# A two-block transformer kernel: heads gated in pairs between mixes, constants made in the down stage, one low half ahead of a head pair

## What is computed

```
# first block
y_att = (_rms(o, subln_w[l]) * (1.0 - lambda_init)).reshape(b, lp, ATT_V)
y_conv = u @ w_conv_out[l]
m = jax.nn.sigmoid(g_att) * y_att + jax.nn.sigmoid(g_conv) * y_conv
h = h + m @ w_out[l]
...
h = h + (jax.nn.silu(gate) * val) @ w_down[l]
# second block
lb_all = jnp.cumsum(jax.nn.softmax(hgrn_lb_logits, axis=0), axis=0)
fg = lbh + (1.0 - lbh) * jax.nn.sigmoid(heads(f, dk))
...
o = o * lax.rsqrt(jnp.mean(o * o, axis=-1, keepdims=True) + EPS)
o = o.reshape(B, S, H * dv) * norm_g
o = o * jax.nn.silu(og)
y_b = o @ w_br_hgrn[l]
```

## Time and profile before

| | |
|---|---|
| median of 3 runs | 1180.97 us |
| the profiled execution's own time | 1181.03 us |
| its span | 1179.4 us |
| TensorE busy | 1134.6 us, 96% of the span |
| VectorE, GpSimd, ScalarE busy | 61%, 55%, 51% |
| chain of waits that ended last, by engine | PE 75%, DVE 10%, issue 7%, POOL 5%, ACT 3% |
| mean granted clock of TensorE | 0.988 |

### The profile page before, as it was taken

The page is one execution under the profiler, slowest core; times in us unless marked ns, Lnnn a source line. Parts: engine busy times, 40 slices in busy tenths (PEclk is TensorE's granted clock), DMA queues, the critical chain, the costliest instruction groups (busy, mean ns, idle before and its releaser), DMA issues.

```text
span 1179.4 us, 24897 instructions
## 1 busy us (share of the span) xinstructions
PE 1134.6 (96%) x8962; PEld 1092.2 (93%) x8962; DVE 720.4 (61%) x1364; ACT 600.3 (51%) x1112; POOL 651.6 (55%) x453
## 2 busy tenths in 40 slices
PE   6999999999889999999899999999999999999997
PEld 6999999998779999999899989898989989999996
DVE  5675766789647777426775757666666546444322
ACT  5654444455256666437545455554635455444332
POOL 5666767660255666544753637364475437656642
PEclk9999999999989999999999999999999999999998
DMA  8444443441344555543432423333445425555541
GB/s 325 144 154 141 171 141 143 143 152 69 142 179 144 178 178 178 199 159 108 178 143 109 142 107 115 134 129 122 160 161 179 143 103 184 181 181 202 185 143 36
DMA packets 26209, 179.43 MB, mean 152 GB/s; under 512 B 2848, under 2 KB 4128, under 8 KB 4768
## 3 DMA queue, kind: packets, MB, share of 16 engines
q1 hardware_dynamic: 25856, 178.28, 42.1%
q10 hardware_dynamic: 288, 0.27, 0.1%
HBM read 177.49 MB, written 1.05 MB: 151 GB/s over the span
## 4 chain that ended last, share of the span: by engine, by line
PE 75%; DVE 10%; issue 7%; POOL 5%; ACT 3%; DVEq 0%; DMA 0%; POOLq 0%; ACTq 0%
PE ps L570 50%; PE ps L852 10%; POOL parts L415 3%; PE ps L930 2%; PE ps L636 1%; DVE ps L2186 1%; DVE act L1824 1%; PE ps L485 1%; ACT parts L1130 1%; DVE branch L1965 1%; PE ps L923 1%; POOL sq L2316 1%; PE ps L610 1%; POOL res L2411 1%; DVE work L1731 1%
## 5 line engine op out<-in xcount | busy, mean ns | idle before, releaser
L415 POOL TENSOR_TENSOR parts<-ring,parts 128x1024 fp32r<-128x1024 f32 x208 | 513.8, 2481 | 468.7 <-ACT parts L1130 465.8
L570 PE MATMUL ps<-x_high,parts 128*128 128x256 f32 (+2 forms) x3088 | 418.0, 284 | 4.3 <-POOL parts L415 2.2
L570 PEld LDWEIGHTS ps<-x_high,parts 128*128 128x128 f32 x3088 | 387.5, 189 | 15.5 <-issue 7.1
L1130 ACT ACTIVATE parts<-ring 128x1024 fp32r<-128x1024 f32 x324 | 323.9, 1049 | 138.3 <-PE ps L852 69.3
L415 DVE TENSOR_TENSOR parts<-ring,parts 128x1024 fp32r<-128x1024 f32 x116 | 152.6, 1315 | 127.3 <-ACT parts L1130 127.3
L570 PE MATMUL ps<-x_low,parts 128*128 128x256 f32 (+2 forms) x1520 | 214.5, 284 | 0.0
L570 PEld LDWEIGHTS ps<-x_low,parts 128*128 128x128 f32 x1520 | 196.3, 189 | 0.0
L1751 DVE SCALAR_TENSOR_TENSOR ps<-glu,table_sb,ps 128x256 f32<-128x256 f32 x232 | 93.3, 481 | 0.6 <-DVE ps L1751 0.3
L852 PE MATMUL ps<-act_high,parts 128*128 128x256 f32 x704 | 87.8, 279 | 0.0
L852 PEld LDWEIGHTS ps<-act_high,parts 128*128 128x128 f32 x704 | 85.1, 188 | 0.0
L570 PE MATMUL ps<-parts,x_high 128*128 128x256 f32 x448 | 62.3, 285 | 0.9 <-DVE work L2099 0.9
(11 more groups left out here) (333 smaller groups left out, 1602.2 us busy)
## 6 DMA issues: line engine op xcount, KB each, us to landing
ring<-weights SPq DMA_DIRECT2D x166, 1024.0 KB, 4.8
res<-h_in SPq DMA_DIRECT2D x4, 272.0 KB, 3.6
act<-mem SPq DMA_DIRECT2D x1, 1024.0 KB, 14.6
out<-xT SPq DMA_DIRECT2D x4, 256.0 KB, 2.4
table_sb<-table SPq DMA_DIRECT2D x1, 969.5 KB, 8.9
table_sb<-table ACTq DMA_DIRECT2D x1, 132.5 KB, 3.5
work<-positions ACTq DMA_DIRECT2D x1, 128.0 KB, 5.5
```

What stands on the lines that cost most here:

```text
L415: eng.tensor_tensor(parts[:, LOW - HIGH + p, cols], ring[:, slot, cols], parts[:, p, cols].bitcast(F32), ALU.subtract)\
L570: mm = pe.matmul(out, left(k), right(k), start=step_ == 0 and k == 0, stop=step_ == 2 and k == KB - 1)
L1130: sc.activation(parts[:, p, cols], ring[:, slot, cols], ACT.Copy).then_inc(split_high, 1)
```

## The change

Three parts. (1) `gate_heads` is split into `root_heads` (the reciprocal) and `gate_heads` (the two multiplications), both for any number of heads. Heads 0 to 3 stay as they were; heads 4 and 5, then 6 and 7, are done in pairs, the reciprocal and the multiplications of a pair at different places between the mixes. (2) The constants and the exponential leave `tables1` and `tables2` and become `constants2` and `bound_exps`, given to `down_low` and `down_high`. (3) In the second block `low_b(2)` stands ahead of `gate_b(3)`.

```
@@ ScalarE, tables2
+            def bound_exps():
+
                 sc.wait_ge(consts_ready, 2)
                 sc.activation(lb_t[:, 0:16], lb_t[:, 0:16], ACT.Exp).then_inc(lb_exp, 1)
...
-            down_high("down1")
+            down_high("down1", bound_exps)
@@ VectorE, gating
-            def gate_heads(g):
-                heads = att[:, 4 * g:4 * g + 4, :].rearrange("p h t -> p (h t)")
-                r_g = att_root[:, g, :]
+            def root_heads(first, count):
+                r_g = att_root[:, first // 4, first % 4 * TQ:(first % 4 + count) * TQ]
                 step(ve.reciprocal(r_g, r_g))
+
+            def gate_heads(first, count):
+                heads = att[:, first:first + count, :].rearrange("p h t -> p (h t)")
+                r_g = att_root[:, first // 4, first % 4 * TQ:(first % 4 + count) * TQ]
                 step(ve.scalar_tensor_tensor(heads, heads, sub_w, r_g, ALU.mult, ALU.mult))
...
             ve.wait_ge(bank_read[7], 1 + 4 * 4 + 1 + 1)
-            gate_heads(0)
-            for t in range(KB):
-                if t == 2:
-                    ve.wait_ge(bank_read[7], 1 + 4 * 4 + 1 + 2)
-                    gate_heads(1)
-                ve.wait_ge(att_gated, t // 4 + 1)
+            root_heads(0, 4)
+            gate_heads(0, 4)
+
+            def mix(t):
+                ve.wait_ge(att_gated, (1, 1, 1, 1, 2, 2, 3, 3)[t])
...
+            mix(0)
+            mix(1)
+            low_mixed1(0)
+            ve.wait_ge(bank_read[7], 1 + 4 * 4 + 1 + 2)
+            root_heads(4, 2)
+            low_mixed1(1)
+            mix(2)
+            gate_heads(4, 2)
+            low_mixed1(2)
+            mix(3)
+            root_heads(6, 2)
+            low_mixed1(3)
+            mix(4)
+            gate_heads(6, 2)
+            low_mixed1(4)
+            for t in range(5, KB):
+                mix(t)
+                if t > 5:
                     low_mixed1(t - 1)
             low_mixed1(KB - 1)
@@ VectorE, constants
+            def constants2():
+
                 l0, l1 = col("lb_logits", 0, KB), col("lb_logits", KB, KB)
...
-            down_low("down1")
+            down_low("down1", constants2)
@@ VectorE, second block
             gate_a(range(4, 6))
+            low_b(2)
             gate_b(3)
-            low_b(2)
             gate_a((6,))
```

More of the change, by code:

```diff
@@ L1819, in _ @@
             add_squares("conv", xT, TQ)
-            def gate_heads(g):
-                heads = att[:, 4 * g:4 * g + 4, :].rearrange("p h t -> p (h t)")
-                r_g = att_root[:, g, :]
+            def root_heads(first, count):
+                r_g = att_root[:, first // 4, first % 4 * TQ:(first % 4 + count) * TQ]
                 step(ve.reciprocal(r_g, r_g))
+            def gate_heads(first, count):
+                heads = att[:, first:first + count, :].rearrange("p h t -> p (h t)")
+                r_g = att_root[:, first // 4, first % 4 * TQ:(first % 4 + count) * TQ]
                 step(ve.scalar_tensor_tensor(heads, heads, sub_w, r_g, ALU.mult, ALU.mult))
-                ve.scalar_tensor_tensor(heads, gates[:, 4 * g:4 * g + 4, :].rearrange("p h t -> p (h t)"), 1.0, heads,
+                ve.scalar_tensor_tensor(heads, gates[:, first:first + count, :].rearrange("p h t -> p (h t)"), 1.0, heads,
                                         ALU.add, ALU.mult).then_inc(att_gated, 1)
@@ L1851, in _ @@
                 ve.tensor_tensor(z, z, att[:, t, :], ALU.add).then_inc(mixed, 1)
-                if t >= 1:
+            mix(0)
[16 more added lines that the diff above has]
+                if t > 5:
                     low_mixed1(t - 1)
```

## The result

| | before | changed |
|---|---|---|
| five runs each, median | 1180.97 us | 1174.54 us |
| lowest and highest | 1179.75, 1182.16 | 1172.21, 1178.66 |
| ratio, 95% interval | | 0.9942 [0.9918, 0.9966] |
| all runs of the study, 45 and 18, median | 1182.1 us | 1173.3 us |

The change is faster, by 6.4 us (0.6%) in these runs and by 8.8 in the wider count; the interval of the ratio leaves out 1. Forecast were 10.6 us, with 1168.4 to 1173.8 as the range: the first median lies 0.7 us above it, the wider one within it, at its slow end. The five runs of the changed kernel lie 6.5 us apart, those of before 2.4. Their times go roughly with the mean granted clock: 1178.66 at 0.985, 1174.54 and 1174.32 at 0.989, 1175.64 at 0.990, 1172.21 at 0.991. The profiled execution is the first of these, the slowest of the five.

The account below looks back on a forecast made before the run. TensorE's chain of waits, 75% of the span, was taken to bound the kernel. Removing idles and their clock drops gave 5.2 + 4.0 + 1.4 = 10.6 us, so 1181.0 - 10.6 = 1170.4 us, range 1168.4 to 1173.8.

Parts of the forecast that it names:

- the places: First block's conv_out tiles, the projection behind them, second block's branch_b: TensorE idles there shrink or go, 10.6 us together.
- the sum: Gains at the three stages added, 5.2 + 4.0 + 1.4 = 10.6 us, and taken off 1181.0 us.
- the signs that the prediction named for being wrong: Any stretch at 0.50 clock left between 297 and 333 or at 868 us, or TensorE waiting near 503.
- A: Gating by pairs in the first block's conv_out tiles: TensorE's 3.48 us idle and its 1.7 us drop go; 5.2 us.
- the draw: VectorE's first paired multiplication (issued 292.77) against GpSimd's first subtraction (292.78) in the gating; VectorE taken to go first.
- rival 1: GpSimd goes first at 292.8 in the gating; TensorE waits 1.5 to 1.7 us before the projection, time 1172.0; chance 0.27.
- B: Constants and exponential moved to the down stage: the projection's 2.34 us TensorE idle and 1.7 us drop go; 4.0 us.
- the drop: TensorE at 1.2 instead of 2.4 GHz behind an idle of 2.3 us or more, costing 1.7 us more.
- B's price: Down stage, fifth chunk: VectorE's low half ends at 500.9 to 501.9, TensorE asks at 502.9; hidden, with 1 us left.
- the row: ScalarE's profiled table load: 1.28 us, exponential 0.02 after it, preferred to the skill's 2.66 us per switch.
- C: Second block's branch_b, low_b(2) first: the 2.76 us wait becomes idles of 1.2 and 1.5; 1.4 us.
- Rival 2: An idle of 2.3 us or more moves instead of going, or branch_b's two idles bring a drop; 1173 to 1175; chance 0.14.

Follow-up runs that it names:

- c_only: Kernel before with only low_b(2) put ahead of gate_b(3) in the second block; 1181.06 us, ratio 0.9992 to the kernel before.
- after_2: Changed kernel repeated unedited, in the first job; 1173.24 us, ratio 0.9917 to the kernel before.
- after_4: Changed kernel repeated unedited, in the third job; 1172.24 us, ratio 0.9923 to the kernel before.
- shared_low: Changed kernel plus VectorE making one of the two low halves of branch_b's second chunk, instead of GpSimd; 1173.0 us, ratio 0.9918 to the kernel before.

## Why the prediction was right in its mechanisms and wrong in its number

**The step that failed** is the one from the places to the time: the sum took everything outside the three stages as it was in one execution of before, and the range gave this no width. The three places took out 10.3 us in the profile, 0.3 less than forecast, while the rest of the same execution came out 7.9 us longer. The first median misses the forecast by 4.1 us: 0.3 are the places, 1.5 lie between the 10.3 us of the stages and the 8.8 of the wider count, and 2.4 between the 8.8 and the 6.4 of the first runs. None of the signs that the prediction named for being wrong appeared: no half clock up to the norm or at the second block's gating, no wait in the down stage. They test the places only.

**A, forecast 5.2, measured 4.8.** Every step stands: no idle between tiles 4 and 5, reciprocals of 3.37 us (3.4), the draw won by VectorE, the second multiplication behind GpSimd (2.73; the prediction had 2.9). The tiles end 28.6 us after they begin, at 309.52; before they took 34.0. That is 5.4, but the projection's first matmul now waits 0.23 us for ScalarE's high part of a mixed tile (L1302), where before its record overlapped the end of the last tile's by 0.35, so that from start to start 4.8 are left. I had not looked at what is late next at that seam on ScalarE. (Two slips in the working have no effect: 291.6 + 0.35 + 0.8 is 292.75, not 292.77, and rival 1's wait begins at 1.4 us, not 1.5.)

**Rival 1 is excluded** in this kernel: it would have shown L1830 at 2.8 us. It is 0.04 us from being true.

**B, forecast 4.0, measured 4.3, 3.3 or 2.6.** No wait on L1130 is left and TensorE runs to the last tile. But the 1.7 us for the drop are there only in the executions in which the kernel before had it: two of three profiles of the old code (27.54, 27.36; 26.53 without it, in c_only). And beside A the idle would have been 1.8 us and, in the one profile of it, without a drop. The stage's gain is a difference to the particular execution that the sum was made against.

**B's price, forecast nothing.** Right, and to the tenth: with the program 6.4 us ahead, the forecast has the fifth chunk's low half end at 494.5 to 495.5 and TensorE ask for it at 496.5. It ended at 495.4 (494.15 + 1.23), and TensorE's product began at 496.5 without a wait. The first instruction behind the exponential stood for GpSimd as allowed for (0.93 against 0.17). One ahead of it did so too, which the prediction didn't have (L1938, 2.36 against 0.16 for L1914 in the earlier trace rows), and it cost nothing, since VectorE then waited 4.36 for the exponential anyway. On the exponential behind the table load the row was right again: it starts 0.01 us after the load. The Trainium skill, "ScalarE: Activation LUTs", What ACT_TABLE_LOAD costs, adds a drain of some 1380 ns, which no run here shows.

**C, forecast 1.4, measured 1.2.** Idles of 1.41 and 1.40 us for the 1.2 and 1.5 reckoned, no drop behind them in any of the seven profiles that had the pair. Together they are as long as the wait that they replace (2.81 against 2.76), so what C gains is the drop, and 0.5 of its 1.7 us goes elsewhere in the stage.

**Rival 2** (an idle moves) did not happen at the three places.

**The sum, forecast 10.6.** Worked out place by place it was 10.3. "Forecast: 1181.0 - 10.6" then takes all other stages as they were. They are not: their total went from 1089.5 to 1098.9 us over fourteen profiles, and the profile of before, at 1091.0, was among the low ones. The mean of the four profiles of the changed kernel is 1094.0, 2.7 above before's two. What can be read of it are drops, up to 1.7 us each, behind short idles that bring one in one execution and not in another; the order of VectorE and GpSimd (1.8 us); and the first weights, for which ScalarE waits up to 1.3 us at the start. Over whole runs the clock's share of the gain can be read from the mean clock of each: the runs of the kernel before lose (1 - clock) times the span, 15.9 us on average in the first job, those of after_2 10.7, 5.2 us less; in the third job before and after_4 lose 15.3 and 10.9. So 5.2 and 4.4 us of a gain of 9.3 and 9.5 (in the means) are clock, where the forecast had three drops, 5.1, and 4.1 and 5.1 are all else, where it had 5.5. The five runs of the result lose 13.1, some 2.3 us more than the later ones, and their mean is 2.5 us longer: the first result fell short of the later ones by its clock.

**The range was too narrow.** It had bounds for costs and none for scatter, though the prediction itself put what a measurement can tell from no change at 2.4 us. The kernel before shows a standard deviation of 1.6 us over 45 runs, the changed one of 2.5 over 18. The median of five of these alone can be off by over a microsecond, and 1174.54 was 1.2 above the wider 1173.3. The three runs shown of before lay within 1.7 us and hid it, and they were themselves 1.1 below the wider median of 1182.1.

**What stays open.** The three stages give 10.3 us in every profile and the wider comparison 8.8. The 1.5 us between them are about one drop. Some 0.4 of it is B's drop, which one of three profiles of the old projection lacks (27.14 us in the mean, not 27.54). The norm ahead of the first up stage is a candidate: all four profiles of the changed kernel have two drops there, both of the kernel before have one, and norm and up stage take 136.6 to 137.1 us against 136.0 and 136.1. But c_only, whose edit comes 500 us later, has two there as well, and 137.1 us, so the change is not needed for it; and shared_low, with the whole change and a further edit 500 us later, has one, and 136.0 us. And the edit that filled the norm's idles took the drops away in two profiles of three and moved the time by no more than its scatter. Where the rest of the 1.5 us goes is not shown. The difference of the means over 45 and 18 runs is 8.9 us with a standard error of 0.6 (from the two deviations above), so what is left of it may be nothing but chance.

## What to carry to other kernels

When a change takes idles away at places that the profile shows, check each place in the next profile by its stage's length, and read the total separately: here the places of the changed kernel repeated within 0.2 us while the rest of it moved by 8.5. Before you give a range, take the spread of repeated runs and of the clock in them as a term of it, and count a gain that comes from a drop in clock only in the share of executions that have the drop. Here a second profile of the kernel before looked much like the first (88.3 and 88.4 us, 1091.5 and 1091.0), and it was a profile with an edit elsewhere that showed the missing drop: two are few for this.

## What the runs showed of the hardware that was not expected

- **The same idle with and without a drop.** 2.32 and 2.34 us of TensorE idle at the same instruction had half clock behind them, 2.33 us had none. 2.75 and 2.76 us had it four times of four, 3.5 to 3.6 us four of four, two of 1.4 us 3.6 apart in none of seven profiles. At the wait for VectorE's L2000 or L2024, 2.0 to 2.3 us had none in twelve profiles and 3.8 us had one in both others. A drop costs up to 1.7 us. The Trainium skill, "TensorE: Matmul & The Clock Gate", What's actually happening, says that the same kernel measures different counts of matmuls at half clock from run to run, by the gate's phase at the kernel's start; the profiles here agree in that the clock varies between executions of one kernel, with 3 to 8 drops in four of them.
- **Small instructions also stand for GpSimd.** An elementwise maximum of 128x8 on VectorE (L1938), issued 0.15 us after GpSimd's subtraction of 128x1024 at 483.78, took 2.36 us and ended with it; the next of its size took 0.17. By the Trainium skill, "SBUF — State Buffer", Who interferes with whom, whoever issues first keeps the shared port to its end, whatever the size of the other's work; this row agrees. The price of losing such a draw (0.04 to 0.2 us apart in three places here) is the rest of the other engine's instruction.
- **Halved gating work is no dearer.** Reciprocals of 128x516 took 3.37 us against 6.59 for 128x1032 in the earlier trace rows, so two of them cost 0.15 us more than the one.
